# Pool sums and layer norm moved between the short convolutions, conditioning pieces in other slots, two conditioning blocks consumed early

## The reference, cut to what matters

```python
mod = silu(c) @ ada_w + ada_b                 # 9 conditioning rows x 6144
sh1, sc1, g1, sh2, sc2, g2 = split(mod, 6)
h = rms_norm(x, norm1_g) * (1 + sc1) + sh1
z = h @ w_in                                  # 1024 x 1792
u_pool, v_conv, g_conv, x_lru, g_lru = split(z)
o_pool = pool_mixer(...)   # windowed means of u_pool (prefix sums), minus u_pool, @ pool_w, * scale
o_conv = conformer_conv(.) # v*sigmoid(g), 31-tap depthwise conv, layer norm, silu
o_lru  = rglru_mixer(...)  # 4-tap conv, two gates, linear recurrence, * gelu(g_lru)
x = x + g1 * (concat(o_pool, o_conv, o_lru) @ w_out)
h = rms_norm(x, norm2_g) * (1 + sc2) + sh2
x = x + g2 * moe_ffn(h)                       # top 4 of 32 experts, 3 MB x 4 of weights each
y = rms_norm(x, final_g)
```

## Time and profile before

| | us |
|---|---|
| three timed runs | 1352.21, 1357.33, 1359.20 (median 1357.33) |
| the profiled execution | 1352.83 |
| its span | 1351.1 |
| PE busy | 1256.2 (93%) |
| DVE / ACT / POOL busy | 287.0 / 198.4 / 110.4 |
| DMA moved | 486.43 MB, mean 360 GB/s |

### The profile page before, as it was taken

One profiled execution on the slowest core, in us unless ns is written; L12 is line 12 of the kernel. 1 busy time (PEld: TensorE's weight loads), 2 busy tenths in 40 slices (PEclk: granted clock), 3 DMA queues, 4 the chain that ended last, 5 costly groups with the idle time before them and its releaser, 6 DMA issues.

```text
span 1351.1 us, 19196 instructions
## 1 busy us (share of the span) xinstructions
PE 1256.2 (93%) x8190; PEld 560.7 (41%) x8190; DVE 287.0 (21%) x562; ACT 198.4 (15%) x347; POOL 110.4 (8%) x176
## 2 busy tenths in 40 slices
PE   2899977968999999999999999999999999999976
PEld 1686955843333333333333333333333333333322
DVE  0651585576100100000000000001001010001027
ACT  3513243220010000000000001001001000100012
POOL 3010022010000000100001100000001001000000
PEclk9999988968999999999999999999999999999978
DMA  9551479379999999999999999999999999999974
GB/s 317 194 160 32 156 246 350 138 312 403 348 403 420 421 422 421 408 409 422 407 407 420 420 415 421 421 420 403 419 417 420 421 421 421 420 422 421 422 299 183
DMA packets 95076, 486.43 MB, mean 360 GB/s; under 512 B 13649, under 2 KB 21852, under 8 KB 45302
## 3 DMA queue, kind: packets, MB, share of 16 engines
q1 hardware_dynamic: 83306, 461.15, 84.9%
q0 software_dynamic: 8608, 20.82, 4.1%
q10 hardware_dynamic: 3076, 3.22, 0.8%
HBM read 470.26 MB, written 18.04 MB: 361 GB/s over the span
## 4 chain that ended last, share of the span: by engine, by line
PE 81%; DMA 8%; DVE 5%; SPq 3%; ACTq 1%; ACT 1%; issue 1%; POOL 0%; DVEq 0%; POOLq 0%
PE psum L1897 61%; PE psum L1570 5%; PE psum L1565 3%; PE psum L1566 3%; PE psum L1567 3%; DMA raw<-in_moe_w_gate 2%; DMA raw<-in_moe_w_down 2%; SPq L481 2%; PE psum L1887 2%; DMA bd_x<-in_lru_wx 1%; ACTq L755 1%; PE psum L1719 1%; DMA raw<-in_w_out 1%; PE psum L2018 1%; DMA xrow<-h_scratch,gidx 1%
## 5 line engine op out<-in xcount | busy, mean ns | idle before, releaser
L1897 PE MATMUL psum<-raw,aT 128*64 128x512 f32 (+1 forms) x1728 | 301.2, 533 | 4.0 <-DMA raw<-in_moe_w_down 3.8
L1897 PE MATMUL psum<-raw,xb 128*64 128x512 f32 (+1 forms) x1920 | 304.0, 512 | 0.3 <-DMA raw<-in_moe_w_gate 0.3
L1897 PE MATMUL psum<-raw,xa 128*64 128x512 f32 x1280 | 283.5, 595 | 0.0
L1491 DVE TENSOR_SCALAR act_t<-psum 128x512 f32<-128x512 f32 (+1 forms) x46 | 28.4, 642 | 873.5 <-PE psum L1897 873.5
L1897 PEld LDWEIGHTS psum<-raw,xb 128*64 128x64 f32 (+1 forms) x1920 | 100.4, 126 | 189.0 <-issue 175.0
L1897 PEld LDWEIGHTS psum<-raw,aT 128*64 128x64 f32 (+1 forms) x1728 | 98.3, 129 | 187.8 <-issue 166.7
L1897 PEld LDWEIGHTS psum<-raw,xa 128*64 128x64 f32 x1280 | 88.2, 137 | 169.7 <-issue 169.7
L979 ACT ACTIVATE glu<-psum 128x512 f32<-128x512 f32 (+1 forms) x46 | 24.2, 559 | 291.6 <-PE psum L1897 291.6
L661 POOL DMA_INDIRECT xrow<-h_scratch,gidx x24 | 27.5, 1145 | 464.4 <-PE psum L1570 430.4
L1565 PE MATMUL psum<-hT_hi,w_hi 128*128 128x260 f32 x208 | 59.4, 286 | 0.0
L1566 PE MATMUL psum<-hT_lo,w_hi 128*128 128x260 f32 x208 | 58.9, 283 | 0.0
(11 more groups left out here) (399 smaller groups left out, 923.6 us busy)
## 6 DMA issues: line engine op xcount, KB each, us to landing
raw<-in_moe_w_gate SPq DMA_DIRECT2D x128, 1024.0 KB, 26.3
raw<-in_moe_w_up SPq DMA_DIRECT2D x128, 1024.0 KB, 26.9
raw<-in_moe_w_down SPq DMA_DIRECT2D x128, 1024.0 KB, 26.8
raw<-in_ada_w SPq DMA_DIRECT2D x24, 1024.0 KB, 9.2
raw<-in_w_in SPq DMA_DIRECT2D x7, 1024.0 KB, 11.6
x<-in_x_prompt SPq DMA_DIRECT2D x2, 2048.0 KB
raw<-in_w_out SPq DMA_DIRECT2D x4, 1024.0 KB, 14.4
yrow_a<-y_scratch SPq DMA_DIRECT2D x2, 2048.0 KB, 10.6
```

Of the source, the lines that this page charges most:

```text
L1491: v.tensor_scalar(act_t[:, b, 0:bank.shape[1]], bank, 8.0, -6.0, ALU.min, ALU.max).then_inc(u_done, 1)
L1897: last = mm(out[w * g4:w * g4 + w, :], x, weights[:, 8 * w * g4:8 * w * g4 + 8 * w], start=start, stop=stop)
```

## The change

It moves work, adds none and drops none. DVE does `pool_sums(0)` behind `after_root(0)`, `pool_sums(1)` between `short_conv(2)` and `(3)`, and `normalize` ahead of `lru_out(0)`; `scale_rows(5)` stands beside `scale_rows(4)`. PE does conditioning blocks 4 and 5 around `gates(1)`, in banks 2 and 3 (`mod_bank`), and ACT copies their rows ahead of `roots(0)`. The conditioning pieces get other slots, so that four are loaded ahead of the last three pieces of `w_in` in the count of used pieces, and the loads of `w_out` mix with the last conditioning pieces. On ACT the two Tanh of the layer norm (L921) now stand ahead of `roots(2)`. The low parts of the last two `w_out` pieces are made by POOL, not DVE.

```diff
+USE = ([("ada", i) for i in range(ADA_A)] + [("in", i) for i in range(4)] + [("mod", i) for i in range(4)]
+       + [("in", i) for i in range(4, WIN)] + [("mod", i) for i in range(4, ADA_B)] + [("out", i) for i in range(WOUT)])
-SLOT = ([0, 1, 2, 3, 4, 5, 6, 7] + [0, 1, 2, 3, 4, 0, 1] + [2, 3, 4, 5, 6, 7, 0, 1, 2, 3, 4, 5, 6, 7, 0, 1]
-        + [2, 3, 4, 0])
+SLOT = ([0, 1, 2, 3, 4, 5, 6, 7] + [0, 1, 2, 3] + [2, 5, 6, 7] + [4, 0, 1]
+        + [3, 5, 6, 7, 2, 4, 0, 1, 5, 6, 7, 1] + [3, 2, 4, 0])
+LOADS = [("mod", i) for i in range(13)] + [("out", 0), ("mod", 13), ("mod", 14), ("out", 1), ("out", 2), ("mod", 15), ("out", 3)]
@@ POOL, behind the 32 small DMAs @@
+            for c in C_OUT[2:4]:
+                g.wait_ge(hi_done, split_no(c) + 1)
+                g.tensor_tensor(w_lo[:, SLOT[c], :], raw[:, SLOT[c], :], hi_slot(c).bitcast(F32), ALU.subtract)\
+                    .then_inc(lo_pool, 1)
@@ ACT @@
             gates(0)
             gates(1)
+            ada_rows(0)
+            ada_rows(1)
             roots(0)
             roots(1)
...
             gates(3)
-            roots(2)
-            roots(3)
-            ada_rows(0)
             for m in range(2):
                 act.wait_ge(ln_pre, m + 1)
                 ac.activation(W[:, 8 + m, :], W[:, 6 + m, :], ACT.Tanh, scale=0.5).then_inc(ln_sig, 1)
-            ada_rows(1)
+            roots(2)
+            roots(3)
+            ada_rows(2)
             for m in range(2):
                 act.wait_ge(pool_ps, m + 1)
                 ac.activation(two(sg_conv[:, m, :]), pair(4 + 2 * m), ACT.Copy, scale=cvp(34, m)).then_inc(pool_in, 1)
-            ada_rows(2)
             ada_rows(3)
@@ DVE @@
             after_root(0)
+            pool_sums(0)
             center()
             after_root(1)
             short_conv(2)
+            pool_sums(1)
             short_conv(3)
+            normalize()
             lru_out(0)
             lru_out(1)
-            pool_sums(0)
-            pool_sums(1)
-            normalize()
             before_root(2)
             before_root(3)
             split_conv()
             after_root(2)
             lru_out(2)
             scale_rows(4)
+            scale_rows(5)
             after_root(3)
             lru_out(3)
-            scale_rows(5)
             split_pool()
-            for i in range(WOUT):
-                lo(C_WOUT + i)
+            for c in C_OUT[0:2]:
+                lo(c)
@@ PE, z_tiles @@
+                    if z == 9:
+                        pe.wait_ge(ada_ev, 6)
@@ PE @@
             gates(0)
+            ada_block(4, C_MOD[0])
             gates(1)
+            ada_block(5, C_MOD[2])
             z_tiles(4)
...
-            for n in range(8):
-                ada_block(4 + n, C_ADAB + 2 * n)
-                if n == 0:
+            for n in range(2, 8):
+                ada_block(4 + n, C_MOD[2 * n])
+                if n == 2:
                     pool_mix(0)
                     pool_mix(1)
```

More of the change, by code:

```diff
@@ L39 @@
 WOUT = 4
-C_WIN, C_ADAB, C_WOUT = ADA_A, ADA_A + WIN, ADA_A + WIN + ADA_B
-C_MOE = C_WOUT + WOUT
+USE = ([("ada", i) for i in range(ADA_A)] + [("in", i) for i in range(4)] + [("mod", i) for i in range(4)]
+       + [("in", i) for i in range(4, WIN)] + [("mod", i) for i in range(4, ADA_B)] + [("out", i) for i in range(WOUT)])
+NO = {piece: n for n, piece in enumerate(USE)}
+C_IN, C_MOD, C_OUT = ([NO[kind, i] for i in range(count)] for kind, count in (("in", WIN), ("mod", ADA_B), ("out", WOUT)))
+SPLIT = C_IN + C_OUT
+C_MOE = len(USE)
 NBUF = 18
@@ L437, in _ @@
             for i, w in enumerate(WIN_ORDER):
-                load(C_WIN + i, win[:, :, 256 * w:256 * w + 256])
+                load(C_IN[i], win[:, :, 256 * w:256 * w + 256])
             sp.wait_ge(mix_done, 1)
@@ L443, in _ @@
                         .then_inc(stack_sp, 16)
[L444 to L450, removed]
+            for kind, c in LOADS:
+                kh, n = slice(4 * (c % 2), 4 * (c % 2) + 4), c // 2 + (4 if kind == "mod" else 0)
+                load(NO[kind, c], (ada if kind == "mod" else wout)[:, kh, n * 512:(n + 1) * 512])
+            sp.wait_ge(chunk_used, C_OUT[0])
             sp.dma_start(x2[:, 0:TT - 1, :], x_prompt[0].rearrange("(t p) d -> p t d", p=P)).then_inc(x2_loaded, 16)
@@ L745, in hi @@
                 if split_no(c) >= R_HI:
-                    before = c - R_HI if c < C_WOUT else c - R_HI - ADA_B
-                    act.wait_ge(chunk_used, before + 1)
+                    act.wait_ge(chunk_used, SPLIT[split_no(c) - R_HI] + 1)
                 ac.activation(hi_slot(c), raw[:, slot, :], ACT.Copy).then_inc(hi_done, 1)
@@ L859, in gates, with ada_rows @@
                 link(ac.activation(W[:, 2 + j, :], W[:, 2 + j, :], ACT.Tanh, scale=sp_2[:, m:m + 1], bias=sp_2[:, m:m + 1]))
+            def ada_rows(n):
+                act.wait_ge(chunk_used, C_MOD[2 * n + 1] + 1)
+                if n >= 2:
+                    act.wait_ge(mod_out[n % 2], 64 * (n // 2))
+                ac.activation(modst[:, n % 2, :], mod_bank(n)[:, 0:P], ACT.Copy).then_inc(ada_ev, 1)
             def roots(m):
@@ L907, in _ @@
             gates(3)
-            roots(2)
-            roots(3)
-            def ada_rows(n):
-                act.wait_ge(chunk_used, C_ADAB + 2 * n + 2)
-                if n >= 2:
-                    act.wait_ge(mod_out[n % 2], 64 * (n // 2))
-                ac.activation(modst[:, n % 2, :], bk[n % 2][:, 0:P], ACT.Copy).then_inc(ada_ev, 1)
-            ada_rows(0)
             for m in range(2):
@@ L1603, in chunk @@
             def chunk(c):
-                pe.wait_ge(lo_done, split_no(c) + 1)
+                if c in C_OUT[2:4]:
+                    pe.wait_ge(lo_pool, C_OUT.index(c) - 1)
+                else:
+                    pe.wait_ge(lo_done, split_no(c) + 1)
                 return hi_slot(c), w_lo[:, SLOT[c], :]
             def ada_block(n, c):
-                outs = [bk[n % 2][32 * j:32 * j + NC, 0:P] for j in range(4)]
+                bank = bk[n % 2] if n < 4 else mod_bank(n - 4)
+                outs = [bank[32 * j:32 * j + NC, 0:P] for j in range(4)]
                 if n == 0:
@@ L1793, in project_samples @@
                 for kk in range(KC):
-                    parts = [chunk(C_WOUT + 2 * n + kk // 4) for n in range(2)]
+                    parts = [chunk(C_OUT[2 * n + kk // 4]) for n in range(2)]
                     for hl in range(2):
```

51 lines of the change are left out of this document (28 added, 23 removed).

## The result

| | median us | runs | lowest to highest | profiled span |
|---|---|---|---|---|
| before, same chip | 1352.58 | 6 | 1350.5 to 1359.2 | 1351.1 |
| changed | 1342.53 | 6 | 1340.82 to 1346.55 | 1339.0 |

The ratio is 0.9918, with a 95% interval of [0.9891, 0.9945]: 10 us faster by the medians, 0.8%. The forecast of 1342 us meets the time, but partly by luck: the six runs of the kernel before are the three that the prediction had (median 1357.3) and three more, from 1350.5 to 1353.0, and the median of the six is 1352.6 us. The gain itself was forecast at 13.0 us and is 10.

A forecast was written before the change was run, and what follows sets the result against it. The start of the output projection was taken to bound the end: 14.3 us earlier minus 1.3 us gives 13.0 off 1352.8, 1339.8 us; halfway up the 4.5 us to the runs' median gives 1342 us, range 1335 to 1351 us.

The forecast's parts named there:

- What counts is the start of the projection: Output projection, begun at 220.67 us: whatever comes before the experts' phase moves the kernel's end one for one.
- The 11 to 15 us that I gave for the projection: Main forecast: projection starts 11 to 15 us earlier, time 1339 to 1346 us; chance 0.68.
- Two early blocks on TensorE: Around `gates(1)`: conditioning block 4 costs 0.1 us, block 5 2.3 us, later `z_tiles` shift 2.4 us.
- The new wait in `z_tiles(4)`: TensorE's second tile there, at 140 us, waits for two ScalarE copies that are over by 137 us.
- Pool sums and norm hidden on VectorE: Moved into VectorE's idle time ahead of `center` and `lru_out(0)`: done at 173.0 instead of 189.5 us.
- The count of eight pieces: Behind `gates(3)`, eight remaining conditioning and `w_out` pieces load at 2.65 us each, landing from 185 to 203.6 us.
- the rival in which they take 8 us: Both round trips of conditioning rows take 8 us, last row 6 us later, gain 7 us, 1349 us; chance 0.12.
- GpSimd's subtractions: Two low parts of `w_out` at 4.8 us each, ready at 210.6 and 215.4 us, just in time.
- The 1.3 us that I charged: Allowance at the projection for slower GpSimd subtractions and for GpSimd and VectorE holding each other up.
- The prediction's sentence on the shared port: Cited the skill: VectorE's second port is shared with GpSimd and they block each other; no trace row showed it.
- The sum: Projection 14.3 us earlier minus 1.3 us charged: 13.0 us off 1352.8, giving 1339.8 us.
- the slower case: GpSimd at the projection needs 16 us a piece, 1361 us; gain used up from 12 us a piece; chance 0.03.

The follow-up runs named there:

- pool_late: Changed kernel with eight needless memsets on GpSimd ahead of each of its two subtractions; 1352.2 us, ratio 0.9997 to before.
- changed_again: The changed kernel run once more, unaltered, giving its second profile; 1342.1 us, ratio 0.9919 to before.
- dve_only: Kernel before with only VectorE's new order of pool sums and layer norm ahead of `lru_out(0)`; 1349.7 us, ratio 0.9974 to before.
- late_blocks: Changed kernel with conditioning blocks 4 and 5 back behind the last gates, their row copies moved along; 1358.3 us, ratio 1.0057 to before.
- mods_first: Changed kernel with other slots and load order, the last conditioning pieces ahead of all of `w_out`; 1343.3 us, ratio 0.9919 to before.
- lru_first: Changed kernel with VectorE's two `lru_out` ahead of the normalisation; 1341.1 us in one run, timed again at 1340.4 us, ratio 0.9909 to before.
- rows_early: `mods_first` with ScalarE's last two conditioning rows each one `w_out` piece earlier; 1341.4 us, ratio 0.9922 to before.
- old_dve: Changed kernel with VectorE's old order of pool sums, layer norm and `lru_out` put back; 1350.6 us, ratio 0.9998 to before.

## Why the prediction was right, point by point

**What counts is the start of the projection.** Right, to within some 1.5 us. Its distance fell by 10.2 us, that of the experts by 10.2, the median by 10.1 us. The 11 to 15 us that I gave for the projection are met by the profiled 12.3 us alone, of which 2.2 are luck; by the distances it is 10.2 and 10.9. `pool_late` starts the experts 10.1 us later than changed and is 10.1 slower (against `changed_again`, which ran beside it), `dve_only` 3.5 us earlier than before and 3.7 faster (against 1353.4, the runs of before beside it), `late_blocks` 5.3 later and 6.9 slower (against 1351.5, likewise). `mods_first` is the exception: 1.3 us nearer to the projection, nothing at the experts, with a low clock at the start of the projection.

**Two early blocks on TensorE.** Right: 1.94 us of matmuls at 126.20 and at 130.35, no wait for pieces. The new wait in `z_tiles(4)` did not show.

**Pool sums and norm hidden on VectorE.** Right in place, wrong in one consequence. Reciprocal at 165.16 (forecast near 167), pool sums from 139.84 and 156.17 (142 and 158), less by the 2.2 us that this execution was ahead. I wrote that `normalize` ends at 173.0 and that `lru_out(0)` could write no earlier, hidden to within 0.1 us. That left out the first product of `lru_out(0)`, 0.7 us, which now has to run between the two; and I did not ask who waits for `lru_out` behind it. The third gates do. `lru_first` showed what that was worth: 2.0 to 2.7 us, some 0.8 for the pause and 1.5 for the clock in it, of the 4.2 us by which the projection missed its forecast (80.15 us from the first gates by my sum, 84.3 measured; 3.5 by the second profile).

**Loads and round trips.** The count of eight pieces is right, and 2.65 us each nearly: 8.39 MB in 22 us are 2.75. I had the first load go out at 180.4 and the last piece land at 203.6 us, 23.2 us in all; measured it is 25.5 (first load 180.64, last `w_out` piece used at 206.16). Full rate ends at 204 us, but some of the 16 DMA engines are not through then. SP's queue from 204 to 205.75 us (packets, MB, share of the 16 engines):

```profile
q1 hardware_dynamic: 46, 0.08, 12.4%
```

It has no packet from 205.7 us on, so the piece is usable about 0.5 us behind its last bytes and 2 us behind the end of full rate. The Trainium skill (DMA: Bandwidth & Descriptors, Anatomy of one DMA, written for GpSimd's queue) has it otherwise: most of a transfer's fixed 2 us is the wait for the receipt of its last byte. The trace does not agree for SP's loads, and it decides: most of these 2 us are last bytes that trail. With `lru_first`'s 81.6 us, 1.5 us of the miss are left, about this tail; no run changed it alone. The round trips kept their time (median 5.0 us, before 4.9), the row at 185.59 went without a wait, and the rival in which they take 8 us did not come.

**GpSimd's subtractions.** I took 4.8 us a piece between 3.2 and 6.4, and they take 4.6. The Trainium skill (GPSIMD Engine Reference, section 3.1, Elementwise) has 4497 ns, and the trace agrees: 4606 ns in the mean here, 4.49 and 4.54 us in `pool_late`. The 1.3 us that I charged are nil in the first profile of the changed kernel, where TensorE never waited for GpSimd, and 1.15 us in the second. VectorE took no part in either: it was through at 206.75 and GpSimd began at 208.24 us (209.08 and 210.70 in the second). The fear behind the charge was sound: in `rows_early` VectorE's second piece ran to 209.45 us, GpSimd's first is recorded from 207.91, and its two took 10.53 us. Less the 1.54 us side by side that is 8.99, twice 4.49: these rows fit a GpSimd that stood until VectorE was through (against the 9.17 us of the changed kernel it lost 1.36 of the 1.54 us), and VectorE lost nothing (4.49 us, as in the changed kernel). The Trainium skill (SBUF — State Buffer, SBUF: two separate sides) has it as a lock that the one which starts first holds for its whole instruction, between GpSimd's reads and a VectorE operation with two inputs from that memory, and the trace agrees. The prediction's sentence on the shared port left out for which VectorE operations it holds.

**The sum.** 14.32 - 4.17 = 10.15 for the start of the projection, and 0 instead of 1.3 for GpSimd: 10.2 us instead of 13.0. In the second profile it is 14.3 - 3.5 = 10.8, less 1.15 for GpSimd, of which the distance to the experts shows 0.5. I took the level of the runs halfway up to the first median; it lay 2.5 us lower still for before (1352.58 against 1355.1, the middle of 1352.8 and 1357.3), and the two errors cancelled in the time. That is luck. The times of the rivals are not all reckoned from one level: from 1355.1 us a gain of 7 gives 1348.1 and not 1349, and the slower case was added to 1352.8.

## What to carry to other kernels

When an operation is moved ahead of others on an engine, list who waits for each of those others, not only for the one moved, and what of them used to run in the idle time that is now filled: here a 5.8 us operation pushed a result for which TensorE stood, and the longer pause went with a loss of clock in six of nine profiles. Two waits that stand side by side can be worth less one at a time than together; try them together before giving either up. And with loads issued in order through reused places, the order of places and the order of use are one plan: count the pieces behind the first one that has to wait.

## What the runs showed of the hardware that I had not expected

- The same 128 convolution matmuls took 13.94 us in the changed kernel at a granted clock of 1.00, and 15.37 us before at 0.89; the second profile of the very same changed kernel had 15.64 us at 0.89. One profiled execution is uncertain by that much.
- The last 1 MB piece of a full queue is usable about 2 us after full rate ends, but only some 0.5 us after its last packet. In `late_blocks` as well: 83 GB/s from 220 to 222 us, no packet of SP's queue from 221.6 us on, and the last piece used at 222.00 us.
- A pause of 1.7 us on TensorE never went with a loss of clock at the fourth gates, one of 2.5 to 2.9 us in six of nine profiles; the same kernel place cost 1.5 us more with it.
- `old_dve` has two levels on one chip, 1348.7 to 1352.5 and 1357.7 to 1358.7 us. I did not find out why.
